# Four slots of split weights, each 32 bytes further along a 128-byte grid than the one before

## What is computed

```python
def reference(x, mem, w_in, ..., w_out_2):
    x = first_block(x, mem, w_in, ...)      # mixer (two attentions, two gates), cross attention, SwiGLU
    return second_block(x, norm_g_2, ...)   # three attentions with gates, one output projection

def swiglu(x, w_in, w_out):
    g, u = jnp.split(x @ w_in, 2, axis=-1)
    return (jax.nn.silu(g) * u) @ w_out
```

## Time and profile before

| | |
|---|---|
| median of 3 runs | 2322.28 us (2319.61 to 2326.85) |
| span of the profiled execution, first to last instruction | 2323.2 us |
| TensorE busy, matmuls / weight loads | 97% / 80% |
| VectorE, ScalarE, GpSimd busy | 56%, 45%, 7% |
| mean granted TensorE clock | 0.990 |
| read from HBM | 417.97 MB, 181 GB/s over the span |

### The profile page before, as it was taken

The page is one execution under the profiler, slowest core; times in us unless marked ns, Lnnn a source line. Parts: engine busy times, 40 slices in busy tenths (PEclk is TensorE's granted clock), DMA queues, the critical chain, the costliest instruction groups (busy, mean ns, idle before and its releaser), DMA issues.

```text
span 2323.2 us, 30087 instructions
## 1 busy us (share of the span) xinstructions
PE 2262.6 (97%) x10167; PEld 1852.2 (80%) x10167; DVE 1305.4 (56%) x1571; ACT 1044.2 (45%) x1243; POOL 167.2 (7%) x175
## 2 busy tenths in 40 slices
PE   7999999999999899999999999998999999999999
PEld 6777888888877678878887888776888788888887
DVE  5444655566567665445444444456655565645664
ACT  4443444555434444433444334334445444545643
POOL 1000000001204040000000000004000000200020
PEclk9999999999999999999999999998999999999999
DMA  7655554555855455555665556554556655655555
GB/s 214 205 162 155 170 169 153 180 156 180 272 195 164 156 181 187 178 187 184 195 190 181 181 181 199 176 176 137 177 167 202 191 177 185 208 176 183 175 181 164
DMA packets 216427, 421.11 MB, mean 181 GB/s; under 512 B 15225, under 2 KB 19361, under 8 KB 214433
## 3 DMA queue, kind: packets, MB, share of 16 engines
q1 hardware_dynamic: 213184, 402.31, 55.2%
q0 software_dynamic: 3168, 17.82, 2.2%
HBM read 417.97 MB, written 2.11 MB: 181 GB/s over the span
## 4 chain that ended last, share of the span: by engine, by line
PE 94%; DVE 3%; DMA 1%; ACT 1%; issue 1%; SPq 0%; DVEq 0%; ACTq 0%
PE b_ps L532 88%; PE b_ps L574 1%; PE b_ps L557 1%; PE b_ps L614 1%; DVE b_x_res L1452 1%; PE b_ps L676 1%; DVE b_w_lo L1294 1%; DVE b_x_res L1443 1%; DMA b_stage<-in_w_up 1%; PE b_ps L629 1%; DMA b_stage<-in_w_in 0%; PE b_ps L623 0%; PE b_ps L694 0%; PE b_ps L630 0%; ACT b_nat L964 0%
## 5 line engine op out<-in xcount | busy, mean ns | idle before, releaser
L1294 DVE TENSOR_TENSOR b_w_lo<-b_stage,b_w_hi 128x1024 fp32r<-128x1024 f32 (+1 forms) x762 | 930.2, 1240 | 625.8 <-ACT b_w_hi L937 620.0
L937 ACT ACTIVATE b_w_hi<-b_stage 128x1024 fp32r<-128x1024 f32 (+1 forms) x762 | 793.8, 1054 | 723.6 <-PE b_ps L532 688.9
L532 PE MATMUL b_ps<-b_w_hi,b_x_hi 128*128 128x512 f32 (+1 forms) x2368 | 944.5, 399 | 10.7 <-DVE b_x_lo L1335 8.0
L532 PE MATMUL b_ps<-b_w_hi,b_x_lo 128*128 128x512 f32 (+1 forms) x2368 | 924.7, 390 | 0.0
L532 PE MATMUL b_ps<-b_w_lo,b_x_hi 128*128 128x512 f32 (+1 forms) x2368 | 923.5, 390 | 0.0
L532 PEld LDWEIGHTS b_ps<-b_w_hi,b_x_hi 128*128 128x128 f32 x2368 | 447.6, 189 | 106.9 <-DVE b_x_lo L1335 9.2
L532 PEld LDWEIGHTS b_ps<-b_w_hi,b_x_lo 128*128 128x128 f32 x2368 | 447.0, 189 | 94.4
L532 PEld LDWEIGHTS b_ps<-b_w_lo,b_x_hi 128*128 128x128 f32 x2368 | 447.8, 189 | 88.1
L532 PE MATMUL b_ps<-b_w_hi,b_ff_h 128*128 128x512 f32 x352 | 141.3, 401 | 6.2 <-DVE b_ff_l L1335 6.2
L532 PE MATMUL b_ps<-b_w_lo,b_ff_h 128*128 128x512 f32 x352 | 140.8, 400 | 0.0
L532 PE MATMUL b_ps<-b_w_hi,b_ff_l 128*128 128x512 f32 x352 | 140.5, 399 | 0.0
(11 more groups left out here) (275 smaller groups left out, 1453.5 us busy)
## 6 DMA issues: line engine op xcount, KB each, us to landing
b_stage<-in_w_in SPq DMA_DIRECT2D x336, 512.0 KB, 4.1
b_stage<-in_w_ffn_in SPq DMA_DIRECT2D x176, 512.0 KB, 4.3
b_stage<-in_w_ffn_out SPq DMA_DIRECT2D x88, 512.0 KB, 4.2
b_stage<-in_w_out SPq DMA_DIRECT2D x64, 512.0 KB, 4.2
b_stage<-in_w_up SPq DMA_DIRECT2D x24, 512.0 KB, 3.9
b_stage<-in_w_o_dsa SPq DMA_DIRECT2D x16, 512.0 KB, 4.3
b_stage<-in_w_o_moba SPq DMA_DIRECT2D x16, 512.0 KB, 4.4
b_stage<-in_w_kv_mem SPq DMA_DIRECT2D x16, 512.0 KB, 4.1
```

The costliest lines, as they stand in the source:

```text
L532: ins = mm(ps[:, ACC + r, 0:n], x[:, kt + t, rows], w[:, slot, t, 0:n], start=first and t == 0 and k == 0, stop=last and t == GK - 1 and k ...
L937: act.activation(w_hi[:, slot, :, 0:n], stage[:, slot, :, 0:n], ACT.Copy)\
L1294: dve.tensor_tensor(w_lo[:, slot, :, 0:n], stage[:, slot, :, 0:n], w_hi[:, slot, :, 0:n].bitcast(F32), ALU.subtract).then_inc(sem("lo_done ...
```

## The change

`w_hi` and `w_lo` lose the dimension of the two weight tiles; a slot becomes 1032 elements (4128 bytes) long, of which the first 1024 are used. Slot 0 lies at 0 bytes on the 128-byte grid, slot 1 at 32, slot 2 at 64 and slot 3 at 96, in `w_hi` and `w_lo` alike. Within a slot the second weight tile begins 2048 bytes after the first, so both lie alike. `stage` keeps its form and place. `w_hi` still begins at 32896; `w_lo` begins 128 bytes later than before, and all that comes after it 256 bytes later, which leaves its place on the 128-byte grid as it was. No instruction is added, removed or put elsewhere on any engine, and shapes, loads and waits are the same.

```diff
+WP = GK * NB + 8
...
-        w_hi = sb("w_hi", [P, SLOTS, GK, NB], F32R)
-        w_lo = sb("w_lo", [P, SLOTS, GK, NB], F32R)
+        w_hi = sb("w_hi", [P, SLOTS, WP], F32R)
+        w_lo = sb("w_lo", [P, SLOTS, WP], F32R)
...
+        def slot_of(w, slot, n):
+
+            return w[:, slot, 0:GK * NB].rearrange("p (t n) -> p t n", t=GK)[:, :, 0:n]
...
-                            ins = mm(ps[:, ACC + r, 0:n], x[:, kt + t, rows], w[:, slot, t, 0:n],
+                            ins = mm(ps[:, ACC + r, 0:n], x[:, kt + t, rows], w[:, slot, t * NB:t * NB + n],
...
-                act.activation(w_hi[:, slot, :, 0:n], stage[:, slot, :, 0:n], ACT.Copy)\
+                act.activation(slot_of(w_hi, slot, n), stage[:, slot, :, 0:n], ACT.Copy)\
...
-                dve.tensor_tensor(w_lo[:, slot, :, 0:n], stage[:, slot, :, 0:n],
-                                  w_hi[:, slot, :, 0:n].bitcast(F32), ALU.subtract).then_inc(sem("lo_done"), 1)
+                dve.tensor_tensor(slot_of(w_lo, slot, n), stage[:, slot, :, 0:n],
+                                  slot_of(w_hi, slot, n).bitcast(F32), ALU.subtract).then_inc(sem("lo_done"), 1)
```

## The result

The changed kernel takes 2354.31 us (median of 3 runs, 2354.3 to 2354.68) against 2322.28 us: 1.0138 times the time before, 95% interval 1.012 to 1.0156. That is 32 us slower where +19 us was forecast. It lies inside the range over all cases, 2296 to 2366 us, but just outside the forecast's own range, 2329 to 2353 us. The profiled execution's span grew from 2323.2 to 2352.5 us.

A forecast was written before the change was run, and what follows sets the result against it. The prediction took TensorE's line 532 matmuls to bound the kernel. Terms of +20.0 us (x), -6.8 us (other tiles) and +5.8 us (settling) sum to +19.0 us, giving 2341 us; range over all cases 2296 to 2366 us.

The forecast's parts named there:

- the forecast's own range: 2329 to 2353 us: settling 0 to 11.5 us, and 32 and 96 bytes each 2 cycles either side of the middle.
- What bounds the kernel: TensorE's line 532 matmuls, 9144 in a chain; loads and splits hidden; one nanosecond on each is 9.1 us at the end.
- ScalarE, VectorE, loads: Writing and reading slots at 32, 64 and 96 bytes costs these engines nothing, loads into stage neither: 0 us.
- Something that depends on where the tiles lie: In line 532's dense stretches, tile placement costs 16 cycles, 6.7 ns, of each matmul: 226.6 ns over x, 233.3 over ff.
- the second rival: Line 532: only the stationary tile's own place counts, or the moving one's reads are indifferent; no change, 2322 us; chance 0.17.
- Call d the stationary tile's place minus the moving one's, on the 128-byte grid: Line 532: d is 0 for x (544 cycles), 64 for the rest (560); after, both see every d equally often.
- I take the middle: Line 532: d of 32 and 96 bytes costs 552 cycles, midway between 544 and 560; mean 230.0 ns for all.
- The term for x: About 6000 line 532 matmuls over x_hi and x_lo go from 226.7 to 230.0 ns: +20.0 us.
- The third rival: Line 532: every slot off the grid costs the full 16 cycles; x +30.0 us, settling 11.5 us; 2364 us; chance 0.16.
- -6.8 us: The 2040 line 532 matmuls with other stationary tiles (ff, oh and the like) go from 233.3 to 230.0 ns.
- Settling, +5.8 us: Over x, some 500 slot changes break the short step, 23 ns each or 11.5 us in all; half is taken.
- The dodge: Line 532: unaligned pairs at 32 and 96 bytes avoid a collision of reads, 528 cycles; faster, 2295 us; chance 0.25.

## Why the prediction was right, and where it wasn't

**What bounds the kernel: right.** TensorE's stream of line 532 sets the end nearly one for one; 27.5 of 29.3 us come out of two dense steps times the counts.

**ScalarE, VectorE, loads: right at 0.** 1057 and 1244 ns stand, and the kernel padded by 256 bytes loses nothing.

**"Something that depends on where the tiles lie", and that it is the relative place: right.** The prediction left open which; moving x alone by 32 bytes and moving all by 64 settle it. With them the second rival falls: 64 bytes on x's own place cost nothing when the weights move along, and 128 bytes on w_lo alone cost 1.2%. The Trainium skill, "TensorE: Matmul & The Clock Gate", section "What happens when you issue a matmul", says that loading the next stationary tile takes no read bandwidth from the running matmul. By that alone the distance between the two tiles would not matter; in this stream of float32r matmuls it does, by 6.7 ns on 226.7, and the runs decide.

**"Call d the stationary tile's place minus the moving one's, on the 128-byte grid": this step failed.** The grid has 256 bytes. The prediction saw in the listing that w_lo moved by 128 bytes and wrote the moves off because they kept the 128-byte grid; nothing in the trace of before supported 128 over 256, since its two places, 0 and 64 bytes, look the same on both. The shift that it priced at nothing loses by itself as much as the whole change (1.0135 beside 1.0138), and the 32-byte steps, the only thing that it priced, lose 1.0112 by themselves. The two together lose no more than the larger of them: in these runs a stretch out of the short step takes 231 to 234 ns in the mean, whatever put it out.

**"I take the middle", 552 cycles for 32 and 96 bytes: this term was mis-sized.** 32 bytes cost 233.3 ns and 96 bytes 234.3 ns, the full amount. The term for x was +20.0 us, with the settling +25.8, and measured +29.8 with the settling in it. The third rival's assumption, that every place but one costs the full amount, fits the five uniform distances measured to within 1 ns, though not 192 bytes. Its term for x, +30.0 us from three slots of four at 233.3 ns, is the measured +29.8 by coincidence, since slot 0 isn't at 226.7 ns here nor the rest at 233.3. Its 2364 us is too much by the 11.5 us of settling that it puts on top, which the measured step already holds.

**"-6.8 us" for the other tiles: mis-sized.** By the dense step they come to -2.3 us. They were to gain where slot 2 meets them at d = 0. With the slots' step alone that slot takes 2.75 us over ff; in the changed kernel, where w_lo is 128 bytes off, it takes 2.79 us:

```profile
1054.07 0.39 PE L538 MATMUL b_ps<-b_w_hi,b_ff_h 128*128 128x512 f32 x1
...
1056.86 0.39 PE L538 MATMUL b_ps<-b_w_hi,b_ff_h 128*128 128x512 f32 x1
```

One pair off its place spoils its neighbours here too.

**Settling, +5.8 us: right in kind, its size not shown for this kernel.** In the kernel with the slots' step alone it is 0.04 us for each group at distance 0, more than the 0.023 us of a hook, but only a quarter of the 500 groups over x are at distance 0: some 5 us. In the changed kernel it can't be separated, since no slot there has both w_hi and w_lo at distance 0.

So the direction was right by a sound reading of the dense steps, and that the number came within 13 us was luck. Of the two causes the prediction left one out, which alone costs 32 us, and undersized the other, which alone costs 27 us, at 19. Both errors make the forecast too low, and it is near only because the two causes overlap instead of adding up. The forecast's own range missed the result by 1 us, and it was too wide by its own terms: 2 cycles on two slots of four are 1 cycle in the mean, 3.4 us, which gives 2332 to 2350 us and not 2329 to 2353.

**The dodge: wrong.** Distances of 32 and 96 bytes cost the full amount, no uniform distance other than 0 that was tried fell under 232 ns, and line 833's small addition, with its 8-column tile, says nothing about tiles of 128.

**What stays open.** What the two reads collide in, if that is what they do, why the best distance is 0 and why the step has 32 cycles on top of its columns even then, no run here tells. Which reads meet isn't separated either: a matmul's weights stream while the next stationary tile is loaded, and no kernel moved x_hi without x_lo. Why w_lo alone spoils the whole stream over x, and why the settling takes nine matmuls in one place and five in another, is open too. At a distance of 192 bytes the last nine steps of a slot took 229 ns, less than any dense stretch off distance 0; whether a uniform 192 would keep that wasn't tried.

## What to carry to other kernels

In a stream of matmuls that each load a new stationary tile, look at the distance from start to start for each pair of operand tensors, and compare it between stages at the same granted clock; a difference of a few ns may be nothing but padding. Here stationary and moving tiles have to begin a multiple of 256 bytes from each other, all of them, for the short step. A shift within SBUF (a pad, a new small tile ahead) cost 1.7% when it moved x_hi and x_lo by 32 bytes and 1.2% when it moved w_lo by 128, with no instruction changed. When a change to a layout is judged, list the distances between all operand tensors before and after, not those of the tensor that was edited.

## What the runs showed that I had not expected

- The dense step of a 128x128 by 512 float32r matmul at a granted clock of 1.00 is 226.7 ns at distance 0 and 232.3 to 234.3 ns at the five other distances that whole stretches had, with a period of 256 bytes. At 192 bytes, seen only within slots, it is some 229 ns.
- One of three products off its place (w_lo by 128 bytes) costs nearly as much, 1.012, as all three off theirs (x moved by 128 bytes, 1.0151).
- After a change to distance 0 the stream takes nine matmuls over x and five over ff to come back to the short step.
- 64 bytes less of padding made the tuned kernel 0.5% faster (2312.31 us beside 2322.37), and two other kernels with all tiles at distance 0 confirm it (0.9942 and 0.9946).
